# TensorE's part of the expert loop written out sixteen times; the other engines' loops kept

## The reference

```
def ec_moe(h, lp):
    probs = jax.nn.softmax((xf @ lp["w_router"]).astype(jnp.float32), axis=-1)
    cap = CAPACITY_FACTOR * n // N_EXPERTS
    gate_vals, tok_idx = lax.top_k(probs.T, cap)
    xe = jnp.take(xf, tok_idx, axis=0)
    hid = jax.nn.silu(jnp.einsum("ecd,edf->ecf", xe, lp["w_e_gate"])) * jnp.einsum("ecd,edf->ecf", xe, lp["w_e_up"])
    ye = jnp.einsum("ecf,efd->ecd", hid, lp["w_e_down"]) * gate_vals[..., None].astype(h.dtype)
    y = jnp.zeros_like(xf).at[tok_idx.reshape(-1)].add(ye.reshape(-1, D))
    return y.reshape(B, L, D)
```

## Time and profile before

| | |
|---|---|
| median of 3 runs | 1850.94 us |
| lowest and highest | 1848.95 and 1852.34 us |
| the profiled execution | 1852.01 us |
| its span | 1850.0 us |
| mean granted clock of TensorE | 0.951 |
| TensorE busy | 1727.9 us, 93% of the span |
| VectorE, ScalarE, GpSimd busy | 20%, 10%, 7% |
| data moved | 628.73 MB, mean 340 GB/s |

### The profile page before, as it was taken

One profiled execution on the slowest core, in us unless ns is written; L12 is line 12 of the kernel. 1 busy time (PEld: TensorE's weight loads), 2 busy tenths in 40 slices (PEclk: granted clock), 3 DMA queues, 4 the chain that ended last, 5 costly groups with the idle time before them and its releaser, 6 DMA issues.

```text
span 1850.0 us, 43144 instructions
## 1 busy us (share of the span) xinstructions
PE 1727.9 (93%) x19754; PEld 805.4 (44%) x19754; DVE 376.0 (20%) x695; ACT 185.5 (10%) x295; POOL 135.6 (7%) x204
## 2 busy tenths in 40 slices
PE   6999899799989999989999989998999899999997
PEld 3787568443434343434343434343434343434342
DVE  4422643611010101010101010101010101010103
ACT  4432431200000000000000000000000000000011
POOL 1000010120000000000001010000010101010000
PEclk9999959799999999999999999999999999999999
DMA  8521723999999999999999999999999999999991
GB/s 295 205 74 48 261 84 132 359 399 416 410 402 413 381 401 370 400 372 399 373 399 373 400 372 404 369 403 367 404 368 402 368 402 372 401 373 400 372 372 79
DMA packets 123373, 628.73 MB, mean 340 GB/s; under 512 B 11198, under 2 KB 14099, under 8 KB 106795
## 3 DMA queue, kind: packets, MB, share of 16 engines
q1 hardware_dynamic: 111872, 598.74, 81.9%
q0 software_dynamic: 10256, 23.91, 4.4%
q10 hardware_dynamic: 1050, 2.97, 0.4%
HBM read 609.37 MB, written 16.21 MB: 338 GB/s over the span
## 4 chain that ended last, share of the span: by engine, by line
PE 91%; issue 4%; DVE 2%; DMA 2%; ACT 1%; ACTq 0%; DVEq 0%; POOLq 0%
PE bank L1780 51%; PE bank L1792 16%; PE bank L1794 8%; PE bank L1369 3%; PE bank L1370 3%; PE bank L1371 3%; PE bank L1621 1%; PE bank L1396 1%; PE bank L1617 1%; PE bank L1679 1%; DMA raw<-in_w_out 0%; PE bank L1391 0%; DMA pos_col<-in_pos 0%; DMA xg<-xn_dram,idxG 0%; DVE S L1093 0%
## 5 line engine op out<-in xcount | busy, mean ns | idle before, releaser
L1780 PE MATMUL bank<-ring,xe 128*32 128x352 f32 x12288 | 943.6, 471 | 67.3 <-issue 64.0
L1780 PEld LDWEIGHTS bank<-ring,xe 128*32 128x32 f32 x12288 | 389.2, 113 | 619.4 <-issue 615.0
L1792 PE MATMUL bank<-ring,hidT 128*32 128x512 f32 x2816 | 364.5, 592 | 0.0
L1300 DVE TENSOR_TENSOR hid<-sg,bank 128x1056 f32<-128x1056 f32 x32 | 40.1, 1254 | 921.3 <-PE bank L1780 921.3
L1794 PE MATMUL bank<-ring,hidT 128*32 128x256 f32 x2816 | 214.5, 379 | 0.0
L1794 PEld LDWEIGHTS bank<-ring,hidT 128*32 128x32 f32 x2816 | 87.5, 110 | 214.7 <-issue 214.7
L881 ACT ACT_TABLE_LOAD x16 | 20.5, 1283 | 962.0 <-PE bank L1780 962.0
L1792 PEld LDWEIGHTS bank<-ring,hidT 128*32 128x32 f32 x2816 | 87.5, 110 | 67.0 <-issue 5.5
L643 POOL DMA_INDIRECT acc_dram<-yab,idx_s x15 | 24.3, 1622 | 1137.2 <-DVE yc L1311 1137.2
L1309 DVE SCALAR_TENSOR_TENSOR yab<-bank,gate_cur,gfab 128x512 f32<-128x512 f32 x16 | 12.0, 751 | 329.9 <-PE bank L1794 329.9
L881 ACT ACTIVATE sg<-bank 128x1056 f32<-128x1056 f32 x32 | 33.6, 1051 | 417.3 <-PE bank L1780 417.1
(11 more groups left out here) (262 smaller groups left out, 817.5 us busy)
## 6 DMA issues: line engine op xcount, KB each, us to landing
ring<-in_w_e_gate SPq DMA_DIRECT2D x128, 1408.0 KB, 9.2
ring<-in_w_e_up SPq DMA_DIRECT2D x128, 1408.0 KB, 8.9
ring<-in_w_e_down SPq DMA_DIRECT2D x96, 1536.0 KB, 9.3
ring<-in_w_e_down SPq DMA_DIRECT2D x32, 1024.0 KB, 8.5
raw<-in_w_ada SPq DMA_DIRECT2D x16, 1024.0 KB, 6.5
raw<-in_w_in SPq DMA_DIRECT2D x8, 1024.0 KB, 5.5
ada_f<-in_w_ada SPq DMA_DIRECT2D x4, 1024.0 KB, 16.7
raw<-in_w_out SPq DMA_DIRECT2D x4, 1024.0 KB, 8.8
```

The costliest lines, as they stand in the source:

```text
L1300: nc.vector.tensor_tensor(hid[:, :, :], sg[:, :, :], psum[:, 3:3 + ROW_TILES, 0:GCOLS], ALU.mult).then_inc(hid_done, 1)
L1780: last = nc.tensor.matmul(bank[b][32 * g:32 * g + 32, 0:GCOLS], xe[:, t, c, :], w[:, n, GCOLS * g:GCOLS * g + GCOLS], start=c == 0, stop=c ...
L1792: nc.tensor.matmul(bank[6][r:r + 32, :], hidT[:, ph, t, c, :], w[:, n, 512 * h:512 * h + 512], start=first, stop=stop)
```

## The change

TensorE's code for the experts becomes a straight line: the Python loop writes `expert(i, i == 0)` sixteen times, for i = 0 to 15. Every i is a number then, and so is every value that TensorE waits for. Expert 0 keeps its own order. The loops of SyncE, GpSimd, ScalarE and VectorE stay. The matmuls, their order, the waits and the increments of TensorE are the same; its code for the experts becomes some eight times as long.

```
-            expert(0, True)
-            with pe.Fori(1, EXPERTS) as i:
-                expert(i, False)
+            for i in range(EXPERTS):
+                expert(i, i == 0)
```

## The result

The changed kernel takes 1756.82 us (median of four runs, 1754.52 to 1758.52), the kernel before beside it 1851.64 us; the ratio is 0.9491, 95% interval 0.9475 to 0.9508. The profiled execution took 1758.5 us, its span (first to last instruction) is 1756.4 us. The forecast was 1757.4 by the median and 1758.5 by the profiled execution.

What follows compares the result with a forecast made beforehand. TensorE was taken as the bound (91% of the chain), with idle time at 14 loop jumps and slow clock behind. 97.0 us saved less 3.5 of late weights is 93.5, from 1850.94 to 1757.4 us; range 1750 to 1763, chance 0.70.

Steps and rivals of the forecast that it cites:

- Step 1: TensorE's expert body without a jump, read from expert 1 and its straight boundary: takes 85.18 us.
- Step 2: TensorE's 14 jump boundaries: 97.0 us saved up to the last L1309, 64.0 of them gaps and 33 slow clock.
- Step 3: Whether everything else keeps up at the boundaries: only ring weights come late, 3.5 us taken, bounds 0 and 16.5.
- The growth of the queue: Weight transfers against a gapless TensorE: landings 87.0 us apart, so delay grows by 1.8 us a body.
- the loads' time to landing: Sign to look for in SyncE's weight loads: climbs by 1.8 us a body, to about 38 us.
- The end of the kernel: SyncE's last loads, five tiles and fin_g: 2 to 5 us late, the same queue's lateness, not added.
- Step 4: Fetching TensorE's straight code: costed at nothing, no gain seen; other bound 2.2 MB, 5.4 us of transfers.
- (a): Rival: the queue of weights becomes the bound well before the last expert; 16.5 us late, 1770.4 us; chance 0.20.
- (b): Rival: TensorE's gaps go but the low clock stays, having another cause; 64.0 us saved, 1786.9 us; chance 0.04.
- (c): Rival: the stall before L1780 is a wait the profile can't show, and stays; 1851 us; chance 0.03.
- (d): Rival: never-fetched straight code stops TensorE at each instruction packet; at 1 us each, 1894 us; chance 0.03.

Runs made afterwards that it cites:

- norows: Straight kernel with GpSimd's gathers for experts 1 to 15 and its adding scatters left out; 1752.43 us, ratio 0.9469.
- gap_long: Straight kernel, TensorE waiting at the start of experts 1 to 15 for VectorE's weighing, with three more VectorE operations ahead of it; 1837.69 us.
- tiny: Straight kernel plus a four-turn TensorE loop around one long-fulfilled wait at the start of experts 1 to 15; 1757.10 us, ratio 0.9498.
- loop5: TensorE's loop kept with three turns of five experts each, expert 0 written out, so two back jumps; 1766.89 us, ratio 0.9561.
- hint: Kernel before, TensorE's loop and 14 jumps kept, with the back jump announced ahead by an added instruction; 1778.02 us, ratio 0.9612.
- extra: Straight kernel plus one 0.36 MB transfer on SyncE's queue at the start of each of 15 expert turns; 1769.46 us, ratio 0.9562.
- straight: The changed kernel itself, unaltered, measured and profiled a second time on another occasion (the second profile); 1759.04 us, ratio 0.9503.
- gap_short: Straight kernel, TensorE made to wait at the start of experts 1 to 15 until VectorE has weighed the expert before; 1774.06 us.
- noload: Kernel before, with its loop, but SyncE leaves out weight transfers for experts 1 to 15 and only raises the semaphores; 1805.02 us, one execution.

## Why the prediction was right

**Step 1, a body of 85.18 us.** Right to the digit: in `norows` all 15 bodies take 85.18 us, in the changed kernel those up to expert 12 take 85.2 to 85.3.

**Step 2, 97.0 us saved, of them 64.0 gaps and 33 slow clock.** Right. `norows`, in which nothing but TensorE is a bound, has a lateness of 0.0, so these 97.0 us are gone in it. That the slow clock goes with the gaps was read from one straight boundary (clock 1.00 and 60 records in 4 us, against 0.50 and 28 behind a jump's gap); `gap_long` shows it the other way round, by bringing it back without a jump.

**Step 3, the near miss.** The mechanism was right and the sizes were a little off. With nothing late the forecast's own terms give 1850.9 - 97.0 = 1753.9 us; `norows`, where nothing is late, took 1752.4. The growth of the queue was put at 1.8 us a body from one pair of bodies; over three pairs it is 2.1 (11.6 to 17.8). By the prediction's own formula, with 85.18 + 2.1 = 87.3 between landings, the last weights would be 476.5 + 14 x 87.3 - 1692.0 = 6.7 us late. Measured were 4.9 in this profile, 7.4 in the second one and 1737.13 - 456.38 - 1277.7 = 3.1 in `tiny`; the forecast took 3.5. The late experts were 13 to 15, as said, and 12 to 15 in the second profile. One sign was wrong: the loads' time to landing was to climb to 38 us, and it stops near 32. By then SyncE's issues take long themselves (below), which the prediction did not foresee; that the one stops the other was not tried. The end of the kernel was to be late by 2 to 5 us at most, by the same lateness: DVE's first L1343 starts 2.71 us behind the last L1309 in both kernels, so the last loads held nothing up.

That the profiled execution took 1758.5 us to the digit is in part luck. It was 4.9 us late where the forecast had 3.5, and it had reached its first L1309 at 455.60 where the kernel before had 457.12; the 1.4 us too much and the 1.5 us too little cancel.

**Step 4, fetching.** Costed at nothing, and it cost nothing. But the reason that I gave, that the same code is fetched in either case, was not all: the instruction queue moved 186 packets before and 155 after, 31 fewer, 2.2 for each of the 14 jumps; `loop5` with two jumps has 159, `hint` with its 14 announced ones 173. So there was a small gain where the prediction saw none, 0.51 MB, an estimated 1.2 us of transfers at 412 GB/s in all. From one jump to the next 10 to 12 packets are moved in the kernel before, mostly 11, and 10 in `hint` (once 11). So the body is indeed fetched anew on every turn. That an unannounced jump throws away what had been fetched ahead is my reading; the traces show only the counts and the starts of the packets.

**The rivals.** (a) did not come to pass before expert 13; `extra` shows what it would have looked like, at the price of 0.36 MB a body. (b) falls with `gap_long`, (c) with `loop5`, `hint` and the result itself, (d) with the profile itself: 155 packets and no idle time by issue.

## What to carry to other kernels

A hardware loop with a long body can cost a fetch at every turn: here, with some 2240 TensorE records in the body, 4.6 us with busy DMA engines and 2.2 us with nearly idle ones, and on TensorE the low clock behind it, 2.4 us more. A loop around a single wait cost nothing; where between the two the cost begins was not tried. Written out the long body costs nothing; announcing the jump ahead got back four fifths of the gap; fewer and longer turns divide the cost. Before you close gaps, ask what used them to catch up: here the transfers did, at a body's 87.3 us against TensorE's 85.2, and twelve buffered units were just enough for sixteen experts.

## What was not expected

**SyncE's issues get long when many loads are under way.** With at most four others on their way the issue of a load takes 0.33 to 0.40 us (`straight`, `tiny` and `extra`, from 430 us on); with six and more it takes from 0.33 to 6.7 us in `straight`. In the straight kernel issues get longer from expert 5 on (up to 2.3 us at 800 us) and take up to 7.5 us later. A load of expert 14's turn, issue duration in ns and time to landing in us:

```profile
L444 SPq DMA_DIRECT2D ring<-in_w_e_gate x1: 7550/7550/7550, 1630.1 to 1630.1; - x1
...
DMA to landing us min/median/max: 32.2/32.2/32.2
```

In `norows`, whose loads land in 8.7 us, the issues around 771 us take 0.37 us. Over expert 14 of the straight kernel the rate goes from 412 to 407 GB/s. Whether the one causes the other was not tried. SyncE has nothing else to do here.

**Weight loads spread out, at no cost in the straight kernel.** TensorE's weight loads were busy for 71% of the span, against 44% before, at some 110 ns each in both; the busy time is that of the union. A body's 1120 loads are 123 us in sum; in the 33.6 us of the second profile of the same kernel nearly four ran at a time, in the 79.52 of expert 8 above fewer than two, which I read as the four column groups drifting apart. A body took the same 85.18 us in both. Five bodies of the second profile:

```profile
453.50:879.40 425.90, 425.90 (x5604) 168.10 (x5600) 62.43 (x100) 16.93 (x15) 32.68 (x35) 1.00 1.02 412
```

168.10 us of weight loads in five bodies are 33.6 a body, against 79.52 in expert 8 above. It cost nothing there, where TensorE runs on from one body into the next; in `hint`, where a jump ends every body, the drifted bodies were 0.5 us longer.

**The clock behind the gaps of all runs.** It stayed at 1.00 behind the 14 gaps of 0.7 to 1.7 us in `hint` and the 15 of 1.3 us in `gap_short`; it fell behind 10 of the 14 gaps of 1.9 to 2.5 us in `noload`, and behind all of 3.6 us (`gap_long`) and of 4.3 to 4.8 us (the kernel before). In `noload` it stayed up behind a gap of 2.23 us and fell behind one of 1.95 us, so the length of the gap doesn't decide alone; what else does is open.
